# Two-block transformer kernel: the first input projection on the input without the tokens' factors, with softplus moved to GpSimd

## The chip, the core and the metric

The kernel is one program on one core of a Trainium2 chip. The metric is device time in microseconds of one execution. Engines: PE (TensorE, matrix products), DVE (VectorE), ACT (ScalarE), POOL (GpSimd), SP (SyncE, which here only issues DMAs). Each engine works through its own instructions in order; semaphores join them.

## The reference, cut to what matters

Two blocks run on 256 tokens of width 1024, all in fp32. The part that is touched is the first block up to its output projection:

```python
def rms_norm(x, w):
    xf = x.astype(jnp.float32)
    y = xf * lax.rsqrt(jnp.mean(xf * xf, axis=-1, keepdims=True) + EPS)
    return (y * w.astype(jnp.float32)).astype(x.dtype)

xn = rms_norm(h, mix_norm_w[l])
proj = jnp.einsum('bsd,de->bse', xn, w_in[l])
q, f_logit, i_v, g, lru_x, lru_gate = jnp.split(proj, ...)
# hgrn2_mix
qf = silu(q);  f = lb + (1 - lb) * sigmoid(f_logit);  log_f = log(f);  k = 1 - f
# per chunk of 32 tokens, b = cumsum(log_f):
#   q*exp(b), k*exp(-b), k*exp(b_last - b), scores, state;  then a group norm, times silu(g)
# rglru_mix
r, ig = sigmoid(block products of conv(lru_x));  log_a = -LRU_C * r * softplus(-a_param)
a = exp(log_a);  h = scan(a, sqrt(1 - a*a) * ig * xc);  y = h * gelu(lru_gate)
h = h + einsum('bse,ed->bsd', concat(o_hg, o_lru), w_out)
```

Behind it come a gated feed-forward network, a second block with two kinds of attention, and a mixture of 16384 single-neuron experts, for which each token's chosen rows are gathered from memory. The factor rsqrt(mean(x*x)) of a token multiplies all of that token's products, so it may be applied before a projection or behind it.

## The kernel before

**Layout.** Activations lie with features on the 128 partitions and 256 tokens along the free dimension. `hT` is the input, eight tiles of 128x256. A projection is one product per weight unit: a unit is 128x1024 fp32 (512 KB), eight blocks for the eight input tiles, and gives 128 output features. For precision every fp32 operand is split in two fp32r parts. ACT writes the high part of a unit to `whi` (L1004, `split` in `act`), DVE writes what remains to `ring_lo` (L1484, `split` in `dve`). Tiles are split in the same manner into `xhi` and `xlo`. A unit costs 24 products: eight of high by high (L437), eight of high by the input's rest (L440), eight of the weight's rest by high (L465, L466, or L454 in the first product of a stage).

**What sets the order.** Everything is written out by hand; each engine's program is in `act`, `dve`, `pe`, `pool` and `sync`. Weight units are split ahead by `Lookahead`: `whi` holds six units, so the first six (names `U_f` and the first two of `U_qq`) are split by `fill(1)` to `fill(3)`, and each later pair when `take` is called for a pair that TensorE is through with. A `take(U)` therefore splits the pair that stands three pairs further on: `take(U_f[2:4])` splits `U_qq[2:4]`, `take(U_qq[0:2])` splits `U_lx[0:2]`, and so on. `take` stands in ACT's program and in DVE's, at places of their own, and neither engine goes on before its two splits are issued.

**The stages of the touched part.** (1) ACT squares `hT`, DVE adds six of the squares, TensorE sums over the features (`sums`), ACT makes the token factors `rstd` (L1018, L1023), DVE scales the input to `xn` (L1511), and then both split it (L1029, L1504). TensorE issues filler products (`keep_clock`, L431) before and behind. (2) TensorE runs six gemms of two units each: f 0 and 1 (the forget logits), qq 0 and 1 (queries), lx 0 and 1 (the recurrent branch's input). ACT reads f and qq from PSUM with a sigmoid (L1083, L1087) and lx with a copy (L1105). DVE makes `ff` (L1577), 23 small steps of the softplus of `lru_a` (L1587 to L1598), `kk` (L1600), two memsets for the scan's chunk limits (L1602, L1604), the scan over the logarithm of f (L1610) and the decayed queries and keys, the last of which is `ks` (L1622). (3) TensorE waits for `ks`, transposes it (L554), makes the scores (L562), the token-major product v (L482 to L484), the gates (L594), and then lg 0, lg 1, g 0 and g 1 with the recurrence of the states between them. (4) The recurrent branch ends with `y` (L1693); its four tiles are split into `ahi` (L1150) and `alo` (L1699), with which the output projection begins (`residual`, `first(0)`). Between its first and second pair stands `hg_norm`: two sums (L624) over `sq`, the squares of the other branch's output (L1158).

**SyncE** issues the loads: four pieces of `hT`, constants, the vectors `vv` with all norm weights, then units in the order of use, each when its ring slot is free.

## Time and profile before

| what | value |
|---|---|
| median of 3 runs | 1137.63 us (1137.52 to 1138.79) |
| the profiled execution | 1137.43 us |
| its span (first to last instruction) | 1135.5 us |
| outside the span | 1.9 us |
| granted TensorE clock, mean | 0.978 |
| PE busy | 1018.7 us, 90% |
| DVE busy | 850.7 us, 75% |
| ACT busy | 419.9 us, 37% |
| POOL busy | 289.9 us, 26% |

The span falls in two parts. Up to about 490 us the two blocks are computed, with TensorE busy nearly throughout. Behind that the experts' rows are gathered, and DMA carries 420 GB/s to the end. The touched part is the first 139 us: the first product of the feed-forward network stands at 139.2 us. Shares of busy time say little about it; what counts is when TensorE has nothing to do and whom it waits for.

### The profile page before, as it was taken

How to read it: one execution, taken by the hardware profiler on the slowest of the kernel's cores; microseconds unless marked ns; L12 is line 12 of the kernel's file. 1: busy time of each engine (PE TensorE's matmuls, PEld its weight loads, DVE VectorE, ACT ScalarE, POOL GpSimd, SP SyncE). 2: the span in 40 equal slices, each digit the busy share in tenths (PEclk: the TensorE clock that was granted, in tenths of full speed). 3: DMA queues.
4: the chain of work that ended last, by engine and by line, in shares of the span. 5: the costliest groups of instructions: out<-in, count | busy, mean ns of one | idle time of the engine just before them, and what ended most of it. 6: DMA issues, size and time to landing. Idle time of an engine off the chain costs nothing.

```text
span 1135.5 us, 14403 instructions
## 1 busy us (share of the span) xinstructions
PE 1018.7 (90%) x5146; PEld 711.0 (63%) x5146; DVE 850.7 (75%) x1789; ACT 419.9 (37%) x839; POOL 289.9 (26%) x262
## 2 busy tenths in 40 slices
PE   7999999999999999999999998787867887767896
PEld 7999999999998877966655554233323333223342
DVE  6988699999867984686797776776776677677555
ACT  5646544445356654352322231221221122122121
POOL 0000000000000000144555544444444444445440
PEclk9999999999999999999999999989999999998999
DMA  9633479889828334599999999999999999999995
GB/s 358 223 136 106 149 256 360 329 302 334 308 77 326 138 112 154 224 381 421 422 420 420 422 420 421 422 421 421 421 422 422 421 422 421 422 421 422 420 422 215
DMA packets 68183, 378.61 MB, mean 333 GB/s; under 512 B 7568, under 2 KB 7952, under 8 KB 35600
## 3 DMA queue, kind: packets, MB, share of 16 engines
q0 software_dynamic: 37152, 268.45, 57.0%
q1 hardware_dynamic: 29808, 106.09, 25.4%
q10 hardware_dynamic: 1152, 3.15, 0.8%
q8 instruction: 42, 0.69, 0.3%
q14 instruction: 29, 0.24, 0.1%
HBM read 376.61 MB, written 1.05 MB: 333 GB/s over the span
## 4 chain that ended last, share of the span: by engine, by line
PE 51%; DMA 32%; DVE 11%; ACT 3%; issue 2%; SPq 0%; POOL 0%; DVEq 0%; ACTq 0%; POOLq 0%
DMA ring_sb<-in_peer,idsb 32%; PE pb L437 8%; PE pb L440 8%; PE pb L940 7%; PE pb L943 7%; PE pb L465 5%; DVE ring_lo L1484 2%; PE pb L894 2%; DVE ring_sb L2179 2%; PE pb L655 2%; PE pb L880 2%; PE pb L819 1%; PE pb L466 1%; PE pb L484 1%; PE pb L482 1%
## 5 line engine op out<-in xcount | busy, mean ns | idle before, releaser
L2179 DVE CUSTOM_DVE_ANT_0 ring_sb<-ring_sb,arena 128x1024 f32<-128x1024 f32 x138 | 168.8, 1224 | 73.5 <-DMA ring_sb<-in_peer,idsb 72.2
L940 PE MATMUL pb<-ring_sb,arena 128*128 128x512 f32 x276 | 153.5, 639 | 74.0 <-ACT arena L1418 74.0
L2280 POOL DMA_INDIRECT ring_sb<-in_peer,idsb x136 | 155.8, 1146 | 213.0 <-PE pb L943 190.2
L437 PE MATMUL pb<-xhi,whi 128*128 128x256 f32 x704 | 178.8, 289 | 2.9 <-DVE arena L1913 2.0
L2280 POOL DMA_INDIRECT arena<-in_peer,idsb x38 | 41.6, 1094 | 539.6 <-DVE idsb L2070 475.0
L440 PE MATMUL pb<-xlo,whi 128*128 128x256 f32 x704 | 175.8, 285 | 0.2
L1413 ACT ACTIVATE arena<-arena 128x4 f32<-128x4 f32 (+2 forms) x77 | 15.7, 205 | 432.2 <-DVE arena L2179 432.1
L1484 DVE TENSOR_TENSOR ring_lo<-ring_sb,whi 128x1024 fp32r<-128x1024 f32 x126 | 147.5, 1217 | 11.2 <-ACT whi L1004 11.1
L943 PE MATMUL pb<-ring_sb,arena 128*128 128x512 f32 x276 | 148.8, 622 | 0.0
L940 PEld LDWEIGHTS pb<-ring_sb,arena 128*128 128x128 f32 x276 | 52.0, 200 | 146.6 <-issue 145.5
L437 PEld LDWEIGHTS pb<-xhi,whi 128*128 128x128 f32 x704 | 134.7, 191 | 6.9 <-issue 3.2
L440 PEld LDWEIGHTS pb<-xlo,whi 128*128 128x128 f32 x704 | 134.8, 191 | 2.6 <-issue 1.4
L1004 ACT ACTIVATE whi<-ring_sb 128x1024 fp32r<-128x1024 f32 x126 | 125.3, 1047 | 9.8 <-DMA ring_sb<-in_w_down 8.7
L943 PEld LDWEIGHTS pb<-ring_sb,arena 128*128 128x128 f32 x276 | 55.7, 202 | 72.0 <-issue 72.0
L1418 ACT ACTIVATE arena<-cs,arena 128x128 f32<-128x128 f32 x256 | 83.2, 391 | 19.4 <-DVE arena L2185 19.1
L2179 DVE CUSTOM_DVE_ANT_0 whi_rows<-whi_rows,arena 128x1024 f32<-128x1024 f32 x39 | 47.7, 1224 | 46.9 <-DMA whi_rows<-in_peer,idsb 46.9
L465 PE MATMUL pb<-xhi,ring_lo 128*128 128x256 f32 x546 | 78.3, 283 | 0.1
L465 PEld LDWEIGHTS pb<-xhi,ring_lo 128*128 128x128 f32 x546 | 71.1, 192 | 0.3 <-DVE ring_lo L1484 0.3
L2179 DVE CUSTOM_DVE_ANT_0 arena<-arena 128x1024 f32<-128x1024 f32 x38 | 46.5, 1223 | 23.9 <-DMA arena<-in_peer,idsb 23.5
L940 PE MATMUL pb<-arena 128*128 128x512 f32 x76 | 41.5, 629 | 22.1 <-ACT arena L1418 22.1
L440 PE MATMUL pb<-alo,whi 128*128 128x256 f32 x208 | 58.2, 285 | 0.8 <-DVE alo L1699 0.8
L437 PE MATMUL pb<-ahi,whi 128*128 128x256 f32 x208 | 58.5, 286 | 0.0
(393 smaller groups left out, 1781.8 us busy)
## 6 DMA issues: line engine op xcount, KB each, us to landing
ring_sb<-in_ada SPq DMA_DIRECT2D x48, 512.0 KB, 5.5
ring_sb<-in_w_gu SPq DMA_DIRECT2D x44, 512.0 KB, 6.8
ring_sb<-in_w_in SPq DMA_DIRECT2D x38, 512.0 KB, 7.7
ring_sb<-in_w_down SPq DMA_DIRECT2D x22, 512.0 KB, 5.9
ring_sb<-in_w_out SPq DMA_DIRECT2D x16, 512.0 KB, 3.5
ring_sb<-in_w_q SPq DMA_DIRECT2D x8, 512.0 KB, 4.0
whi_rows<-in_w_q SPq DMA_DIRECT2D x6, 512.0 KB, 9.3
ring_sb<-in_peer,idsb POOLq DMA_INDIRECT x136, 27.2
```

The costliest lines, as they stand in the source:

```text
L437: e.matmul(o, hi_w(u)[:, c], xh(k), start=start, stop=False, skip_group_check=skip)
L440: e.matmul(o, hi_w(u)[:, c], xl(k), start=False, stop=False, skip_group_check=skip)
L465: e.matmul(o, lo_w(u)[:, kc(k)], hi_of(k), start=False, stop=False)
L655: mm = e.matmul(o, lo_w(u)[:, kc(n)], ah_of(k), start=False, stop=False, skip_group_check=True)
L880: mm = e.matmul(pb[b][:, j * 128:(j + 1) * 128], slot(u)[:, kc(k)], xk(k)[:, tile * 128:(tile + 1) * 128], start=k == 0 and j == 0, stop=k ...
L940: mm = e.matmul(pb[4 + 2 * tile][:, :], dgr[col % 8], o[:, 1024:1536], start=begin, stop=end)
L943: e.matmul(pb[5 + 2 * tile][:, :], dgr[col % 8], o[:, 1536:2048], start=begin, stop=end).then_inc(*PU.up(("row", col)))
L1004: e.activation(hi_w(u), slot(u), ACT.Copy).then_inc(*HI.up(u))
L1418: e.activation(dgr[col % 8], c_("ident"), ACT.Copy, scale=ae[:, col:col + 1]).then_inc(*AD.up(("dg", col)))
L1484: e.tensor_tensor(lo_w(u), slot(u), hi_w(u).bitcast(F32), SUB).then_inc(*LOV.up(u))
L2179: e.tensor_tensor_reduce(o, o, h2t[tile], 1.0, 0.0, MUL, ADD, aa[:, col:col + 1]).then_inc(*VD.up(("dot", col)))
L2280: e.indirect_dma_start(rows_at[s], None, peer, bass.IndirectOffsetOnAxis(ap=idsb[:, col:col + 1], axis=0)).then_inc(s_row[s], 16)
```

## The change

- The first six gemms, and v, lg and g, multiply `hT` times the norm weight, without the token factors. Where such a product leaves PSUM, it is multiplied by the token factor: `scaled` on DVE for f, qq, lx, lg and g (one instruction of 128x512 each), and a per-partition scale in ACT's copy for v, for which TensorE turns the factors into token-major form (`rtok0`). ACT's sigmoids for f, qq and g read the scaled copy in SBUF and no longer PSUM; ACT's copies of lx and lg are gone.
- The norm weight `mix` comes in front of the input, in the same load, as `hx`. ACT makes `xhi` by a copy with that scale, DVE makes `xlo` in one instruction. The sums over the squares move into the middle of gemm f 1, and take five products in place of three (DVE adds four squares, not six). The eight filler products behind them are gone; the ten in front stay.
- ACT computes `ff` (before: DVE), and the logarithm ahead of the queries' sigmoids, which now wait for a third table load.
- The softplus steps run on GpSimd, but for one reciprocal on DVE, and so do the memset of `scT` and the two memsets for the scan. DVE's scan waits for the last of these.
- The factor 0.5 of the GELU is folded into the product that gives `y`. The split of `y` stands ahead of both halves of g on ACT and DVE.
- SyncE issues the second part of the constants and the positions four units later.

```diff
-                e.dma_start(half(hT, i), half(xT, i)).then_inc(s_x[i], 16)
+                cols = slice(KD + 512 * i if i else 0, KD + 512 * (i + 1))
+                e.dma_start(hx[:, cols], xT[:, cols]).then_inc(s_x[i], 16)
...
+                        product(o, u, kc(k), k, hi_of, lo_of, k == 0, False, (paced, k) if paced and i == 0 else False)
...
-            sums("n0", (0, 8), (AN, ("n0", "ln")))
+            def first_sums():
+                e.wait_ge(s_cst, 16)
+                sums("n0", (0, 0), (AN, ("n0", "ln")))
+
+            gemm(U_f[0:2], ("f", 0), (VH, ("fx", 0)), paced="n0")
+            gemm(U_f[2:4], ("f", 1), (VH, ("fx", 1)), mid=first_sums)
+            gemm(U_qq[0:2], ("qq", 0), (VH, ("qx", 0)))
+            gemm(U_qq[2:4], ("qq", 1), (VH, ("qx", 1)))
...
-            gemm(U_f[0:2], ("f", 0), (AH, ("sf", 0)), fresh="n0")
-            gemm(U_f[2:4], ("f", 1), (AH, ("sf", 1)))
...
+            b = where["rtok0"] = bank((AN, "rtok0"))
+            e.wait_ge(*AN.at(("n0", "rstd")))
+            for tile in range(2):
+                mm = e.matmul(pb[b][:, tile:tile + 1], rstd[:, tile * 128:tile * 128 + 128], c_("ident")[:, 0:1], start=True, stop=True)
+            mm.then_inc(*PN.up("rtok0"))
...
+            first = la.fill(1)
...
+                e.activation(hi_of(k), hk(k), ACT.Copy, scale=mix[:, k:k + 1]).then_inc(*XHI.up(("n0", k)))
+                if k == 1:
+                    split(first[0:1])
+            split(first[1:2])
+            for k in range(KD):
                 square("n0", k)
+            split(la.fill(2))
+            split(la.fill(3))
...
-            x_hi("n0")
...
             for i in range(2):
+                e.wait_ge(*VH.at(("fx", i)))
+                e.activation(half(sf, i), half(sf, i), ACT.Sigmoid).then_inc(*AH.up(("sf", i)))
+                if i == 0:
+                    e.wait_ge(*VH.at("oml"))
+                e.wait_ge(*AH.at(("sf", i)))
+                for h in (2 * i, 2 * i + 1):
+                    e.activation(one_(ff, h), one_(sf, h), ACT.Identity, scale=oml[:, h:h + 1], bias=lbd[:, h:h + 1]).then_inc(*AH.up(("ff", h)))
                 take(U_f[2 * i:2 * i + 2])
...
-                e.activation(half(sf, i), pb[where["f", i]][:, :], ACT.Sigmoid).then_inc(*AH.up(("sf", i)))
...
             e.activation(lf, ff, ACT.Ln).then_inc(*AH.up("lf"))
+            take(U_qq[0:2])
...
+            e.preload_act_table_set(SIGM)
+            for i in range(2):
+                e.wait_ge(*VH.at(("qx", i)))
+                e.activation(half(qs, i), half(qdec, i), ACT.Sigmoid).then_inc(*AH.up(("qs", i)))
+            take(U_qq[2:4])
...
-                e.activation(half(vtok, tile), pb[where["v"][tile]][:, :], ACT.Copy).then_inc(*AH.up(("v", tile)))
...
+                e.activation(half(vtok, tile), pb[where["v"][tile]][:, :], ACT.Copy, scale=rtok0[:, tile:tile + 1]).then_inc(*AH.up(("v", tile)))
...
+            take(U_g[0:2])
+            e.wait_ge(*VL.at("y"))
...
+                    take(U_g[2:4])
+                e.wait_ge(*VH.at(("gx", i)))
+                e.activation(half(gs, i), half(lg, i), ACT.Sigmoid).then_inc(*AH.up(("gs", i)))
...
+            def scaled(dst, bank_, st_, name):
+
+                rs = one_(rstd, 0).unsqueeze(1).broadcast_to([128, 2, T])
+                e.tensor_tensor(v3(dst, T), v3(pb[bank_][:, :], T), rs, MUL).then_inc(*st_.up(name))
...
+                e.scalar_tensor_tensor(out=lo_of(k), in0=hk(k), scalar=mix[:, k:k + 1], in1=hi_of(k).bitcast(F32), op0=MUL,
+                                       op1=SUB).then_inc(*XLO.up(("n0", k)))
+                if k == 1:
+                    split(first[0:1])
+            split(first[1:2])
...
-            e.memset(scT, 0.0).then_inc(*VH.up("sc0"))
...
+            split(la.fill(3))
+            e.wait_ge(*AN.at(("n0", "rstd")))
+            e.wait_ge(*USED.at(U_f[1]))
+            scaled(half(sf, 0), where["f", 0], VH, ("fx", 0))
+            e.wait_ge(*GL.at("two more"))
+            e.reciprocal(sp_acc, sp_acc).then_inc(*VH.up("softr"))
...
+            e.wait_ge(*USED.at(U_f[3]))
+            scaled(half(sf, 1), where["f", 1], VH, ("fx", 1))
...
-            e.wait_ge(*PN.at("n0"))
-            e.memset(sq[:, 0:1024], 1.0).then_inc(*VH.up("m1"))
-            e.wait_ge(*VH.at("m1"))
-            e.memset(sq[:, 0:1024:CH], 0.0).then_inc(*VH.up("m0"))
...
+            e.wait_ge(*AH.at("lf"))
+            e.wait_ge(*GL.at("m0"))
+            e.tensor_tensor_scan(bb, sq[:, 0:1024], lf, 0.0, MUL, ADD).then_inc(*VH.up("bb"))
+            take(U_f[2:4])
...
+            e.wait_ge(*USED.at(U_qq[1]))
+            scaled(half(qdec, 0), where["qq", 0], VH, ("qx", 0))
+            take(U_qq[0:2])
...
+            e.wait_ge(*USED.at(U_qq[3]))
+            scaled(half(qdec, 1), where["qq", 1], VH, ("qx", 1))
+            take(U_qq[2:4])
+            for i in range(2):
+                e.wait_ge(*AH.at(("qs", i)))
+                e.tensor_tensor(half(qs, i), half(qdec, i), half(qs, i), MUL).then_inc(*VH.up(("qs", i)))
...
+                e.wait_ge(*USED.at(U_lg[2 * i + 1]))
+                scaled(x_, where["lg", i], VL, ("lg", i))
...
-            e.tensor_tensor(th_, th_, gx, MUL).then_inc(*VL.up("y"))
+            e.scalar_tensor_tensor(out=th_, in0=gx, scalar=0.5, in1=th_, op0=MUL, op1=MUL).then_inc(*VL.up("y"))
+            take(U_g[0:2])
...
+                e.wait_ge(*USED.at(U_g[2 * i + 1]))
+                scaled(half(lg, i), where["g", i], VH, ("gx", i))
+                if i == 0:
+                    take(U_g[2:4])
                 e.wait_ge(*AH.at(("gs", i)))
-                e.tensor_tensor(half(gs, i), pb[where["g", i]][:, :], half(gs, i), MUL).then_inc(*VH.up(("gs", i)))
...
+            e.memset(scT, 0.0).then_inc(*GL.up("sc0"))
+            e.wait_ge(*AH.at("su"))
+
+            def soft(ins, name):
+                ins.then_inc(*GL.up(name))
+                e.wait_ge(*GL.at(name))
+
+            soft(e.tensor_scalar(sp_acc, su, 2.0, None, ADD), "two more")
+            e.wait_ge(*VH.at("softr"))
+            soft(e.tensor_tensor(su, su, sp_acc, MUL), "ratio")
...
+            for d in (13, 11, 9, 7, 5, 3, 1):
+                soft(e.tensor_tensor(sp_acc, sp_acc, w2_, MUL), ("times", d))
+                soft(e.tensor_scalar(sp_acc, sp_acc, 1.0 / d, None, ADD), ("term", d))
...
+            soft(e.tensor_scalar(nsp, sp, -LRU_C, None, MUL), "nsp")
+            e.wait_ge(*PN.at("n0"))
+            soft(e.memset(sq[:, 0:1024], 1.0), "m1")
+            soft(e.memset(sq[:, 0:1024:CH], 0.0), "m0")
```

The first place is on DVE, between the first half of `ff` and the transposes' operand `ks`. `arena` holds nearly all tiles of this stage, `sq` the scan's chunk limits; two 128x1024 rows at `ring_lo` are the rests of one pair of units. In the kernel before, at the first half of `ff`:

```order
L1577 TENSOR_SCALAR arena<-arena,small 128x256 [waits s_dve_hgrn,s_act_hgrn]
L1577 TENSOR_SCALAR arena<-arena,small 128x256
L1484 TENSOR_TENSOR ring_lo<-ring_sb,whi 128x1024 [waits s_hi_split] x2
L1577 TENSOR_SCALAR arena<-arena,small 128x256 [waits s_act_hgrn]
L1577 TENSOR_SCALAR arena<-arena,small 128x256
L1587 TENSOR_SCALAR small<-small 128x4 [waits s_act_hgrn]
```

The pair at L1484 is that of qq 1; it stands ahead of the second half of `ff` and of all softplus steps, of which L1587 is the first. Behind the softplus DVE goes on:

```order
L1604 MEMSET sq 128x32 [waits s_dve_hgrn]
L1484 TENSOR_TENSOR ring_lo<-ring_sb,whi 128x1024 [waits s_hi_split,s_dve_hgrn]
L1484 TENSOR_TENSOR ring_lo<-ring_sb,whi 128x1024 [waits s_hi_split]
L1615 TENSOR_TENSOR arena<-pb,arena 128x512 [waits s_act_hgrn]
L1618 TENSOR_TENSOR small<-small,vv 128x8 [waits s_act_hgrn]
L1484 TENSOR_TENSOR ring_lo<-ring_sb,whi 128x1024 [waits s_hi_split] x2
L1610 SCALAR_TENSOR_TENSOR arena<-sq,arena 128x1024 [waits s_act_hgrn]
L1613 TENSOR_TENSOR arena<-arena 128x1024 [waits s_dve_hgrn]
L1615 TENSOR_TENSOR arena<-pb,arena 128x512 [waits s_act_hgrn]
L1620 TENSOR_TENSOR arena<-arena 128x1024 [waits s_act_hgrn]
L1622 TENSOR_TENSOR arena<-arena 128x1024 [waits s_act_hgrn]
```

The pairs here are lx 0 and lx 1, both ahead of the scan (L1610); `ks` is L1622. The same stretch of DVE in the changed kernel:

```order
L1494 TENSOR_TENSOR ring_lo<-ring_sb,whi 128x1024 [waits s_hi_split] x2
L1552 TENSOR_TENSOR arena<-pb,rstd 128x512 [waits s_unit_used,s_act_norm]
L1594 RECIPROCAL small<-small 128x4 [waits s_pool_lru]
L1596 CAST cosT<-arena 128x256 [waits s_pos]
L1598 TENSOR_TENSOR small<-small,vv 128x8 [waits s_act_hgrn]
L1552 TENSOR_TENSOR arena<-pb,rstd 128x512 [waits s_unit_used]
L1603 TENSOR_SCALAR arena<-arena 128x1024 [waits s_act_hgrn]
L1606 SCALAR_TENSOR_TENSOR arena<-sq,arena 128x1024 [waits s_pool_lru,s_act_hgrn]
L1494 TENSOR_TENSOR ring_lo<-ring_sb,whi 128x1024 [waits s_hi_split] x2
L1610 TENSOR_TENSOR arena<-arena 128x1024 [waits s_dve_hgrn]
L1552 TENSOR_TENSOR arena<-pb,rstd 128x512 [waits s_unit_used]
L1494 TENSOR_TENSOR ring_lo<-ring_sb,whi 128x1024 [waits s_hi_split] x2
```

The pair ahead of L1552 is qq 0. That of qq 1 has moved behind the scan (L1606), which waits for GpSimd and for the logarithm, and that of lx 0 is the last row; `ff` is gone from DVE and the reads from PSUM (L1552) have come in.

The second place is on ACT, between the split of `y` (`ahi`) and the logarithm for the group norm's factors (`stdt`). Before:

```order
L1004 ACTIVATE whi<-ring_sb 128x1024 [waits s_slot11,s_unit_used]
L1004 ACTIVATE whi<-ring_sb 128x1024 [waits s_slot12,s_unit_used]
L1150 ACTIVATE ahi<-xn 128x256 [waits s_dve_lru]
L1150 ACTIVATE ahi<-xn 128x256 x3
L1154 ACTIVATE arena<-pb 128x512 [waits s_unit_used]
L1155 ACT_TABLE_LOAD
L1158 ACTIVATE sq<-pb 128x512 [waits s_pe_hgrn]
L1158 ACTIVATE sq<-pb 128x512
L1004 ACTIVATE whi<-ring_sb 128x1024 [waits s_slot13,s_unit_used]
L1004 ACTIVATE whi<-ring_sb 128x1024 [waits s_slot14,s_unit_used]
L1163 ACTIVATE stdt<-pb,cs 128x512 [waits s_pe_hgrn]
```

Both sigmoids of g (L1154) wait for their gemm, and the pair of splits that `take(U_g[2:4])` issues stands at the top. In the changed kernel:

```order
L1159 ACTIVATE ahi<-xn 128x256 [waits s_dve_lru]
L1159 ACTIVATE ahi<-xn 128x256 x3
L1164 ACTIVATE arena<-arena 128x512 [waits s_dve_hgrn]
L1013 ACTIVATE whi<-ring_sb 128x1024 [waits s_slot11,s_unit_used]
L1013 ACTIVATE whi<-ring_sb 128x1024 [waits s_slot12,s_unit_used]
L1164 ACTIVATE arena<-arena 128x512 [waits s_dve_hgrn]
L1165 ACT_TABLE_LOAD
L1168 ACTIVATE sq<-pb 128x512 [waits s_pe_hgrn]
L1168 ACTIVATE sq<-pb 128x512
L1013 ACTIVATE whi<-ring_sb 128x1024 [waits s_slot13,s_unit_used]
L1013 ACTIVATE whi<-ring_sb 128x1024 [waits s_slot14,s_unit_used]
L1173 ACTIVATE stdt<-pb,cs 128x512 [waits s_pe_hgrn]
```

Each sigmoid (L1164) now waits for a DVE instruction, and that pair stands between the two. The third place is the same stretch on DVE. Before:

```order
L1693 TENSOR_TENSOR xn<-xn,sq 128x1024 [waits s_dve_lru]
L1484 TENSOR_TENSOR ring_lo<-ring_sb,whi 128x1024 [waits s_hi_split] x2
L1701 TENSOR_TENSOR arena<-pb,arena 128x512 [waits s_act_hgrn]
L1484 TENSOR_TENSOR ring_lo<-ring_sb,whi 128x1024 [waits s_hi_split] x2
L1699 TENSOR_TENSOR alo<-xn,ahi 128x256 [waits s_x_hi] x4
L1701 TENSOR_TENSOR arena<-pb,arena 128x512 [waits s_act_hgrn]
L1484 TENSOR_TENSOR ring_lo<-ring_sb,whi 128x1024 [waits s_hi_split] x2
L1706 SCALAR_TENSOR_TENSOR arena<-pb,vv,rstd 128x512 [waits s_act_hgrn]
```

The four `alo` rows, for which the output projection waits, stand behind two pairs and one half of g. In the changed kernel:

```order
L1698 SCALAR_TENSOR_TENSOR xn<-sq,xn 128x1024 [waits s_dve_lru]
L1494 TENSOR_TENSOR ring_lo<-ring_sb,whi 128x1024 [waits s_hi_split] x2
L1702 TENSOR_TENSOR alo<-xn,ahi 128x256 [waits s_x_hi] x4
L1552 TENSOR_TENSOR arena<-pb,rstd 128x512 [waits s_unit_used]
L1494 TENSOR_TENSOR ring_lo<-ring_sb,whi 128x1024 [waits s_hi_split] x2
L1709 TENSOR_TENSOR arena<-arena 128x512 [waits s_act_hgrn]
L1552 TENSOR_TENSOR arena<-pb,rstd 128x512 [waits s_unit_used]
L1709 TENSOR_TENSOR arena<-arena 128x512 [waits s_act_hgrn]
L1494 TENSOR_TENSOR ring_lo<-ring_sb,whi 128x1024 [waits s_hi_split] x2
L1714 SCALAR_TENSOR_TENSOR arena<-pb,vv,rstd 128x512 [waits s_act_hgrn]
```

They moved up past one pair and that half; both halves of g now stand behind them, each as a read from PSUM (L1552) and a product with the sigmoid (L1709), with ACT's sigmoid between the two.

## Rows read from the trace of the kernel before

**Rows 1.** The page: PE's busy tenths, the chain's shares, one group of part 5.

```profile
PE   7999999999999999999999998787867887767896
...
PE 51%; DMA 32%; DVE 11%; ACT 3%; issue 2%; SPq 0%; POOL 0%; DVEq 0%; ACTq 0%; POOLq 0%
...
L2280 POOL DMA_INDIRECT ring_sb<-in_peer,idsb x136 | 155.8, 1146 | 213.0 <-PE pb L943 190.2
```

**Rows 2.** Windows: from:to, its length, busy us (count) by engine, PEclk, DMA, GB/s.

```profile
20.70:49.50 28.80, 28.68 (x240) 28.48 (x238) 26.75 (x60) 17.38 (x23) 0.00 (x0) 1.00 0.80 305
...
104.00:109.00 5.00, 4.18 (x35) 3.98 (x34) 5.00 (x8) 2.61 (x5) 0.00 (x0) 1.00 0.53 154
...
139.00:330.00 191.00, 190.92 (x1594) 190.41 (x1592) 169.42 (x214) 89.19 (x127) 0.00 (x0) 1.00 0.80 292
```

**Rows 3.** Timeline of PE, first 15 us: start, length, line, out<-in, count, [idle before].

```profile
5.38 4.64 PE L431 MATMUL pb<-hT 128*128 128x128 f32 x20 [5.38 <-DMA hT<-in_xT]
...
11.18 1.19 PE L496 MATMUL pb<-sq,cs 128*128 128x256 f32 x4
...
14.50 0.36 PE L437 MATMUL pb<-xhi,whi 128*128 128x256 f32 x1 [0.35 <-ACT xhi L1029]
```

**Rows 4.** Timeline of ACT, first 30 us.

```profile
12.40 0.47 ACT L1018 ACTIVATE stdt<-pb,cs 128x256 f32<-128x256 f32 x1 [0.44 <-PE pb L496]
...
19.23 3.89 ACT L1004 ACTIVATE whi<-ring_sb 128x1024 fp32r<-128x1024 f32 x4
...
26.48 1.28 ACT L1079 ACT_TABLE_LOAD   x1
27.78 0.60 ACT L1083 ACTIVATE arena<-pb 128x512 f32<-128x512 f32 x1
```

**Rows 5.** Timeline of DVE, 33 to 46 us.

```profile
33.69 0.16 DVE L1593 TENSOR_TENSOR small<-small 128x4 f32<-128x4 f32 x1
33.89 0.17 DVE L1594 TENSOR_SCALAR small<-small 128x4 f32<-128x4 f32 x1
...
36.90 0.70 DVE L1600 TENSOR_SCALAR arena<-arena 128x1024 f32<-128x1024 f32 x1
37.75 0.91 DVE L1602 MEMSET sq<- 128x1024 f32 x1 [0.16 <-issue]
...
41.16 0.68 DVE L1615 TENSOR_TENSOR arena<-pb,arena 128x512 f32<-128x512 f32 x1
...
44.10 2.28 DVE L1610 TENSOR_TENSOR_SCAN arena<-sq,arena 128x1024 f32<-128x1024 f32 x1
```

**Rows 6.** Timeline of POOL, first microsecond: its only instructions before the gathers.

```profile
0.27 0.10 POOL L2367 MEMSET const-float32-1.0<- 128x1 f32 x1
```

**Rows 7.** Timeline of PE, at the waits for `ks`, for `alo`, and at the group norm's sums.

```profile
50.57 1.09 PE L554 MATMUL pb<-cs,arena 128*128 128x128 f32 x8 [0.55 <-DVE arena L1622]
...
108.70 0.39 PE L440 MATMUL pb<-alo,whi 128*128 128x256 f32 x1 [0.82 <-DVE alo L1699]
...
111.84 1.88 PE L624 MATMUL pb<-sq,cs 128*128 128x512 f32 x4
```

**Rows 8.** Timeline of DVE, 101 to 110 us.

```profile
101.96 1.22 DVE L1693 TENSOR_TENSOR xn<-xn,sq 128x1024 f32<-128x1024 f32 x1
103.09 2.35 DVE L1484 TENSOR_TENSOR ring_lo<-ring_sb,whi 128x1024 fp32r<-128x1024 f32 x2
...
108.23 1.42 DVE L1699 TENSOR_TENSOR alo<-xn,ahi 128x256 fp32r<-128x256 f32 x4
```

**Rows 9.** Timeline of ACT, 103 to 110 us.

```profile
108.81 1.09 ACT L1158 ACTIVATE sq<-pb 128x512 f32<-128x512 f32 x2
```

**Rows 10.** Timeline of PE, two gaps in the gather part.

```profile
736.12 1.10 PE L940 MATMUL pb<-arena 128*128 128x512 f32 x2 [2.63 <-ACT arena L1418]
...
746.05 2.05 PE L940 MATMUL pb<-ring_sb,arena 128*128 128x512 f32 x2 [2.83 <-ACT arena L1418]
```

**Rows 11.** Window behind the second of those gaps.

```profile
745.30:748.70 3.40, 2.65 (x3) 1.18 (x4) 2.50 (x9) 1.28 (x4) 0.54 (x1) 0.51 1.01 422
```

160 lines of the change are left out of this document (56 added, 104 removed).

## The prediction, made before the changed kernel was run

> **What bounds the kernel now.** I read the page first. Its busy tenths of PE and its chain [rows 1] show TensorE full in the first half of the span and the gathers' DMA in the second, so I looked at where the touched part, the first 139 us, leaves TensorE without work. The windows answer it: from 20.7 to 49.5 us it is busy for 28.68 of 28.8 us, at 104 to 109 us it lacks 0.8 us, and from 139 to 330 us it is busy for 190.92 of 191 [rows 2]. The timeline names the gaps: nothing useful before the first weight product at 14.50 us [rows 3], 0.55 us before the transposes at 50.57 us, 0.82 us before the first product with `alo` at 108.70 us [rows 7]. So the stretch behind 14.5 us is bound by TensorE's own work, with ACT and DVE close behind. Since the feed-forward network goes on without a gap and the gathers wait for its results, I carry a shift at 139 us to the end one to one. The profiled execution took 1137.43 us, its span and 1.9 us around it; the median is 0.2 us longer. A measurement of this kernel can tell about 0.2% (2.3 us) from no change.
>
> **The gain at the start.** The ten filler products stay, and end at 10.0 us (5.38 + 4.64) [rows 3]. `xhi`, `xlo` and the first split unit need only the input's first pieces and are there by then, so weight products start at 10.0 instead of 14.5 us: 4.5 us gained. Given back: until about 11.2 us TensorE runs at half speed (there four records of 256 columns begin to take 1.0 us [rows 3], half of what they took before), 0.6 us; and five fp32 sums of 256 columns now stand inside gemm f 1. A 512-column sum takes 0.88 us here (1.88 for two with the tail) [rows 7], so five of half the size take 2.15 us. If nothing waited, the transposes would start near 10.0 + 0.6 + 6 x 5.76 + 2.15 + 0.1 = 47.4 us, 3.2 us earlier than now. (A gemm is 48 products; 240 fill 28.8 us [rows 2], 0.12 us each.)
>
> **The first wait that takes its place.** The rests of qq 1 now stand behind DVE's scan, so I follow the chain to the scan.
> - TensorE: f 0 ends at 16.4, f 1's first unit at 19.2, the sums at 21.5 us with their tail.
> - ACT: logarithm and exponential of the factors 0.47 and 0.45 [rows 4], three exponentials of four columns, by my estimate from DVE's 0.16 us for such a tile [rows 5] 0.35 together: 22.8 us.
> - DVE: four small dependent steps at 0.20 (33.69 to 33.89) [rows 5], 23.5; the pair of qq 0, 2.27 (two of 2.35 with one tail [rows 8]), 25.8; the scaled read from PSUM, 0.68 [rows 5]: 26.5 us.
> - ACT: the sigmoid, 0.60 [rows 4], 27.1; two tiles of `ff`, each priced like the factors' logarithm of the same size, 0.47 less a tail of 0.1, the second sigmoid and two more tiles: 29.2; the high parts of qq 1, 3.89/4 = 0.97 each [rows 4], 31.15; the table load, 1.28 [rows 4], 32.4; the logarithm of 1024 columns, priced like a split unit, 1.05: 33.5 us.
> - DVE: the scan, 2.21 of issue (2.28 with its tail) [rows 5], then qq 1's first rest, 1.22: 37.0 us.
>
> TensorE gets to qq 1 at 30.3 us and has used its high part at 32.2 us. It then stands until 37.0 us: 4.8 us. The 32 products left (3.84) and both lx gemms (11.52) give 52.4 us; with `rtok0` the transposes start at 52.5 us, 1.9 us later than now. `ks` is ready before that (about 44.3 us), so today's 0.55 us wait is gone and hides nothing any more. The high part of lx 1 comes at 46.6 us, just when it is wanted. **Term: +1.9 us.**
>
> **Softplus on GpSimd.** It starts behind DVE's reciprocal at 26.6 us, makes 22 dependent steps and the memsets, and must be through by 33.5 us, or the scan waits, with qq 1's rests queued behind it and TensorE waiting for those. With 1.1 us for the memsets (0.91 on DVE [rows 5]) the limit is (33.5 - 26.6 - 1.1)/22 = 0.26 us a step. No row shows GpSimd arithmetic. Bounds: a one-column memset's 0.10 us [rows 6] from below, which costs nothing; an indirect DMA's 1.15 us [rows 1] from above, 22 x 0.89 = +19.5 us. The nearest row in kind is DVE's 0.20 us [rows 5]; I take half more, 0.30 us, as each step also passes a semaphore. **Term: +0.8 us**, and 2.2 us for each further 0.1 us. What DVE is freed of (23 x 0.2 = 4.6 us, one memset of 0.91 us twice) gains nothing, because DVE then waits for the logarithm.
>
> [...]
>
> **TensorE's clock.** Behind a gap of 2.83 us at 746 us the granted clock is 0.51 in the first window [rows 11], the 1.2 GHz level, and a pair of products takes 2.05 us instead of 1.10; behind a gap of 2.63 us at 736 us it does not fall [rows 10]. A gap of 4.8 us is longer than both. A stretch of 3.4 us at the lower level, as in that window, loses 1.7 us of work; the bounds are 0 and twice that. I take the middle, since TensorE is then dense up to the transposes. **Term: +1.7 us.** The Trainium skill, "TensorE: Matmul & The Clock Gate", part 1, says the throttled state is the default and only activity lifts it; by that rule the fall is certain, by the rows likely, and the sum differs by this term.
>
> **The end of the recurrent branch.** From lg on TensorE is dense again; DVE reads lg with a scale (0.68 us) where ACT copied it (0.60), so `y` keeps its distance. From the start of `y` the sums of the group norm now start 9.9 us later (101.96 to 111.84) [rows 7, 8]: they wait for `alo`, 0.82 us, and the rest of TensorE's work. After the change `alo` comes 2.9 us sooner, and TensorE is through with the first pair about 1 us sooner. But `sq` comes later. From the start of `y`: 1.14, one pair 2.27, four `alo` 1.34, the scaled g 0 0.68 (5.5 in all with the issue overlaps), ACT's sigmoid and the first of two high parts to 7.1, DVE's pair 2.27, the product with the sigmoid 0.60 and the scaled g 1 0.69 to 10.65, sigmoid 0.5, table 1.28 [rows 4] and the square 0.6 [rows 9]: 13.0 us. **Term: +3.1 us**, and a gap of about 4.6 us on TensorE. Behind it ACT has a pair of high parts (1.9 us) queued ahead of the group norm's logarithm; before, that pair was done while ACT waited. The second half of `xlo` then comes 9.7 us behind the sums instead of 8.3. **Term: +1.4 us.** A fallen clock in that gap costs little, as TensorE has slack there: **+0.3 us.**
>
> **Sum:** 1137.43 + 1.9 + 0.8 + 1.7 + 3.1 + 1.4 + 0.3 = 1146.6 us, against the median 1146.8 us.
>
> **The rivals.**
> - The softplus decides (0.15): steps of 0.5 us or more. At 0.6 us the scan waits 7.5 us instead of 0.8: 1153.5 us. For it: 23 instructions with a semaphore each on an engine whose indirect DMAs take 1.15 us. Against: the memsets of 0.10 us.
> - Mild (0.17): a softplus in time and no fallen clock: 1137.6 + 1.9 + 3.1 + 1.4 = 1144.0 us.
> - Faster (0.04): the rests of qq 1 are there when TensorE asks, and `sq` when the first pair is done. Then only 3.2 us at the start and 0.8 us at `alo` count: 1133.6 us. It needs a scan that starts by 32.2 - 1.2 - 2.2 = 28.8 us, before `ff` is whole by my count. For it speaks only that a wait in a hand-written order is easily misplaced by me.
> - No change (0.03): the first wait alone is absent: -3.2 + 3.1 + 1.4 gives 1138.9 us.
>
> **How the numbers follow.** The forecast has 0.61. The range goes from 1142 us, a little under the mild case, to 1154 us, which takes in steps of 0.6 us; about 0.1 is left above and 0.07 below. Faster 0.04, within 0.2% 0.03, slower 0.93.
>
> **What would show it.** Right: weight products from 10 us; a gap of 4 to 7 us on PE inside qq 1, released by DVE's `ring_lo`; scan at 33 to 36 us; transposes near 55 us; a gap of 4 to 5 us before the group norm's sums, released by ACT; the feed-forward network's first product near 148 us. Wrong: scan before 30 us, GpSimd's `m0` far from 34 us, or a shift at 139 us that shrinks in the gather part.

## The result, and the profile after

| | before | after |
|---|---|---|
| median of 6 runs each | 1137.91 us (1137.52 to 1138.79) | 1147.65 us (1146.42 to 1149.13) |
| profiled execution | 1137.43 us | 1147.03 us |
| its span | 1135.5 us | 1145.1 us |
| its mean granted clock | 0.978 | 0.973 |

The change costs 0.84% (ratio 1.0084, 95% interval 1.0074 to 1.0095). The forecast was 1146.8 us in a range of 1142 to 1154, so 0.85 us separate it from the median. The profiled executions lie 9.60 us apart. Both add about 1.9 us to their spans, so the rows can be compared directly.

The page of the kernel after: its part 1, the busy tenths of PE and the chain.

```profile
PE 1023.8 (89%) x5138; PEld 713.1 (62%) x5138; DVE 845.5 (74%) x1758; ACT 420.4 (37%) x840; POOL 298.5 (26%) x288
...
PE   7799899999999999999999998777877877787797
...
PE 43%; DMA 32%; DVE 17%; ACT 4%; issue 3%; POOL 1%; POOLq 0%; DVEq 0%; SPq 0%; ACTq 0%
```

PE's tenths are nearly as full as before [rows 1]; PE's share of the chain fell from 51% to 43%, DVE's rose from 11% to 17%. PE is busy 5 us longer (1023.8 against 1018.7) with no more products (5138 against 5146), which points to the clock. The place of the loss is in PE's timeline (start, length, line, operation, count, idle before it and what ended it):

```profile
5.88 4.63 PE L435 MATMUL pb<-hx 128*128 128x128 f32 x20 [5.88 <-DMA hx<-in_xT]
10.17 0.56 PE L441 MATMUL pb<-xhi,whi 128*128 128x256 f32 x1
...
30.97 0.35 PE L441 MATMUL pb<-xhi,whi 128*128 128x256 f32 x1 [0.86 <-ACT whi L1013]
...
38.15 1.86 PE L469 MATMUL pb<-xhi,ring_lo 128*128 128x256 f32 x7 [5.05 <-DVE ring_lo L1494]
...
55.44 1.07 PE L563 MATMUL pb<-cs,arena 128*128 128x128 f32 x8
...
119.88 3.63 PE L633 MATMUL pb<-sq,cs 128*128 128x512 f32 x4 [4.79 <-ACT sq L1168]
```

Against [rows 3, 7]: the weight products start at 10.17 instead of 14.50 us. Then TensorE waits 0.86 us for the high part of qq 1, stands 5.05 us in the middle of qq 1's first unit for `ring_lo` from DVE, and starts the transposes at 55.44 us, 4.87 us later than before. It stands again, for 4.79 us, before the group norm's sums (L633), for ACT's squares. The windows (from:to, length, busy us and count by engine, PEclk, DMA, GB/s) show what follows each gap:

```profile
38.10:41.50 3.40, 3.35 (x15) 3.35 (x16) 3.40 (x4) 1.10 (x2) 0.00 (x0) 0.50 0.10 17
...
120.00:123.40 3.40, 3.40 (x5) 1.32 (x6) 2.21 (x2) 3.31 (x5) 0.00 (x0) 0.50 0.00 0
148.00:330.00 182.00, 181.61 (x1508) 181.02 (x1507) 162.86 (x197) 83.02 (x117) 0.00 (x0) 1.00 0.84 307
```

In 38.1 to 41.5 us TensorE is busy for 3.35 us and does 15 products; the clock is at 0.50, its 1.2 GHz level. The same in 120.0 to 123.4 us. From 148 us on it is dense, as before [rows 2]. DVE, ACT and GpSimd around the first gap:

```profile
29.91 0.69 DVE L1603 TENSOR_SCALAR arena<-arena 128x1024 f32<-128x1024 f32 x1 [2.60 <-ACT arena L1101]
34.69 2.29 DVE L1606 TENSOR_TENSOR_SCAN arena<-sq,arena 128x1024 f32<-128x1024 f32 x1 [4.09 <-POOL sq L2290]
36.90 2.33 DVE L1494 TENSOR_TENSOR ring_lo<-ring_sb,whi 128x1024 fp32r<-128x1024 f32 x2
```

```profile
29.78 1.99 ACT L1013 ACTIVATE whi<-ring_sb 128x1024 fp32r<-128x1024 f32 x2
...
33.08 1.06 ACT L1105 ACTIVATE arena<-arena 128x1024 f32<-128x1024 f32 x1
```

```profile
26.61 0.20 POOL L2277 TENSOR_TENSOR small<-small 128x4 f32<-128x4 f32 x1 [3.49 <-DVE small L1594]
...
30.11 0.57 POOL L2282 TENSOR_SCALAR small<-small 128x4 f32<-128x4 f32 x1
...
33.43 0.95 POOL L2289 MEMSET sq<- 128x1024 f32 x1
```

DVE makes `kk` at 29.91 us, then waits 4.09 us for GpSimd's mask, scans at 34.69 us, and only then makes the rests of qq 1 (L1494, x2). At the end of the branch ACT and DVE read so:

```profile
112.52 2.00 ACT L1013 ACTIVATE whi<-ring_sb 128x1024 fp32r<-128x1024 f32 x2
...
117.84 1.28 ACT L1165 ACT_TABLE_LOAD   x1
119.13 1.08 ACT L1168 ACTIVATE sq<-pb 128x512 f32<-128x512 f32 x2
120.10 2.00 ACT L1013 ACTIVATE whi<-ring_sb 128x1024 fp32r<-128x1024 f32 x2
122.00 0.69 ACT L1173 ACTIVATE stdt<-pb,cs 128x512 f32<-128x512 f32 x1
```

```profile
106.51 1.22 DVE L1698 SCALAR_TENSOR_TENSOR xn<-sq,xn 128x1024 f32<-128x1024 f32 x1
...
116.47 0.68 DVE L1552 TENSOR_TENSOR arena<-pb,rstd 128x512 f32<-128x512 f32 x1
...
129.00 0.76 DVE L1720 TENSOR_TENSOR xlo<-arena,xhi 128x256 fp32r<-128x256 f32 x2 [0.48 <-ACT xhi L1180]
```

All the profiled executions side by side. "qq 1" is the start of its first product, "distance" from there to the transposes, `y`, "sums" and `xlo` the starts of DVE's `y`, of the group norm's sums and of the second half of `xlo`, "FFN" the first product of the feed-forward network; all in us of the span. The last column is the median of the timed runs.

| kernel | qq 1 | transposes | distance | `y` | sums | `xlo` | FFN | median |
|---|---|---|---|---|---|---|---|---|
| before | 32.20 | 50.57 | 18.37 | 101.96 | 111.84 | 119.82 | 139.23 | 1137.9 to 1138.3 |
| after | 30.97 | 55.44 | 24.47 | 106.51 | 119.88 | 129.00 | 148.45 | 1147.65 |
| e12_fill_gap | 30.06 | 53.16 | 23.10 | 104.22 | 117.59 | 126.71 | 146.46 | 1145.22 |
| e2_limits_first | 31.09 | 55.48 | 24.39 | 106.53 | 119.90 | 129.02 | 148.79 | 1145.34 |
| e13_ten_steps | 30.39 | 57.83 | 27.44 | 108.91 | 122.27 | 131.40 | 150.84 | 1149.33 |
| e1_rests_early | 30.18 | 52.86 | 22.68 | 103.92 | 117.29 | 126.41 | 146.37 | 1145.61 |
| e3_early_limits | 31.36 | 51.80 | 20.44 | 102.85 | 116.22 | 125.33 | 145.46 | 1143.59 |
| e7_start | 31.25 | 49.10 | 17.85 | 100.18 | 113.54 | 122.66 | 142.07 | 1140.59 |
| e5_squares_first | 31.25 | 55.98 | 24.73 | 107.04 | 115.66 | 128.55 | 150.28 | 1148.46 |
| e10_end2 | 30.16 | 55.61 | 25.45 | 106.68 | 115.30 | 125.06 | 145.11 | 1143.64 |
| e11_both2 | 30.07 | 47.91 | 17.84 | 98.98 | 107.61 | 117.35 | 137.39 | 1137.53 |
| e14_early_clock | 30.21 | 48.06 | 17.85 | 99.11 | 107.73 | 117.48 | 138.54 | 1136.47 |
| e15_both3 | 30.04 | 47.88 | 17.84 | 98.95 | 107.57 | 117.22 | 136.61 | 1135.76 |
| e16_before_gpsimd | 32.14 | 49.42 | 17.28 | 100.34 | 110.22 | 118.19 | 137.61 | 1136.39 |

Two remarks for reading it. From the same code TensorE reaches qq 1 at 30.04 to 30.39 us in some executions and at 30.97 to 31.36 us in others, so differences of a step are taken from the distances and not from single clock times. And the median of five runs is only good to about 1 us for these kernels, whose runs lie 1.6 to 3.6 us apart and were not timed side by side with the kernel after; where a few tenths are at stake, the rows decide.

### The profile page after: what moved, and what is told of

It reads as the page before. It is cut to its first block, busy times and chain, and to the rows that moved or that the text cites. A ratio compares the mean times of both kernels' runs of the same rounds, so it can differ in the third digit from the quotient of the medians.

```text
span 1145.1 us, 14390 instructions
## 1 busy us (share of the span) xinstructions
PE 1023.8 (89%) x5138; PEld 713.1 (62%) x5138; DVE 845.5 (74%) x1758; ACT 420.4 (37%) x840; POOL 298.5 (26%) x288
## 4 chain that ended last, share of the span: by engine, by line
PE 43%; DMA 32%; DVE 17%; ACT 4%; issue 3%; POOL 1%; POOLq 0%; DVEq 0%; SPq 0%; ACTq 0%
DMA ring_sb<-in_peer,idsb 21%; PE pb L949 8%; DMA xn<-in_peer,idsb 7%; PE pb L952 7%; PE pb L441 5%; PE pb L444 5%; DVE ring_lo L1494 5%; PE pb L469 3%; DMA ring_sb<-in_peer,halves 2%; PE pb L903 2%; DVE arena L1756 2%; DVE ring_sb L2188 1%; PE pb L889 1%; PE pb L828 1%; PE pb L664 1%
## 5 line engine op out<-in xcount | busy, mean ns | idle before, releaser
L949 PE MATMUL pb<-ring_sb,arena 128*128 128x512 f32 x276 | 150.4, 627 | 71.2 <-ACT arena L1428 71.1
L2312 POOL DMA_INDIRECT ring_sb<-in_peer,idsb x136 | 151.9, 1117 | 205.2 <-PE pb L952 183.5
L1494 DVE TENSOR_TENSOR ring_lo<-ring_sb,whi 128x1024 fp32r<-128x1024 f32 x126 | 147.9, 1219 | 16.8 <-ACT whi L1013 16.6
L952 PE MATMUL pb<-ring_sb,arena 128*128 128x512 f32 x276 | 148.4, 621 | 0.0
L1013 ACT ACTIVATE whi<-ring_sb 128x1024 fp32r<-128x1024 f32 x126 | 125.2, 1046 | 12.9 <-DMA ring_sb<-in_w_down 9.2
L469 PE MATMUL pb<-xhi,ring_lo 128*128 128x256 f32 x560 | 81.4, 285 | 5.4 <-DVE ring_lo L1494 5.4
L469 PEld LDWEIGHTS pb<-xhi,ring_lo 128*128 128x128 f32 x560 | 73.5, 193 | 5.8 <-DVE ring_lo L1494 5.8
L2188 DVE CUSTOM_DVE_ANT_0 arena<-arena 128x1024 f32<-128x1024 f32 x38 | 46.5, 1224 | 23.8 <-DMA arena<-in_peer,idsb 23.3
```

Source lines behind the costliest of these rows:

```text
L469: e.matmul(o, lo_w(u)[:, kc(k)], hi_of(k), start=False, stop=False)
L949: mm = e.matmul(pb[4 + 2 * tile][:, :], dgr[col % 8], o[:, 1024:1536], start=begin, stop=end)
L952: e.matmul(pb[5 + 2 * tile][:, :], dgr[col % 8], o[:, 1536:2048], start=begin, stop=end).then_inc(*PU.up(("row", col)))
L1013: e.activation(hi_w(u), slot(u), ACT.Copy).then_inc(*HI.up(u))
L1494: e.tensor_tensor(lo_w(u), slot(u), hi_w(u).bitcast(F32), SUB).then_inc(*LOV.up(u))
L2188: e.tensor_tensor_reduce(o, o, h2t[tile], 1.0, 0.0, MUL, ADD, aa[:, col:col + 1]).then_inc(*VD.up(("dot", col)))
```

## The experiments

The theory is that of the prediction: the changed kernel waits at two places because of the order in which DVE, ACT and GpSimd work their queues off, and the clock falls behind both waits. The rivals: the gain at the start is not there in the first place (input later, half speed, sums inside f 1); GpSimd decides; or what is won at one place is lost before the feed-forward network.

### The clock in the first gap

```diff
                         product(o, u, kc(k), k, hi_of, lo_of, ...)
+                    for _ in range(18 if u == U_qq[2] else 0):
+                        e.matmul(pb[7][:, 0:128], c_("ones"), c_("ones"), start=True, stop=True, skip_group_check=True)
                     e.wait_ge(*rest_of(u))
```

> The changed kernel with 18 filler products of 128 columns (0.24 us each, 4.3 us together, on constants into an unused bank; their result is not used) put where TensorE waits for the rests of qq 1, between 32.9 and about 37.3 us. Nothing else moves: the rests still come at 38.15 us. Theory A (the granted clock falls because TensorE stands, and this costs by itself): at full speed up to 41.5 us TensorE does in those 3.41 us twice the work; 1.7 us are won, the transposes start at 53.7 us, the time is 1145.9 us. Theory B (the clock's fall costs nothing since the lx gemms wait for their high parts anyway): within 0.5 us of the changed kernel, 1147.2 us or more.

Measured: 1145.22 us (1144.53 to 1148.04), ratio 1.0069 (1.0055 to 1.0083). PE's timeline in and behind the gap:

```profile
32.04 4.18 PE L468 MATMUL pb<-cs 128*128 128x128 f32 x36
37.25 1.10 PE L471 MATMUL pb<-xhi,ring_lo 128*128 128x256 f32 x7 [1.03 <-DVE ring_lo L1496]
```

The fillers stand in the gap, the rests come 7.19 us behind qq 1's first product as they did without fillers (7.18 us), the next seven products take 1.10 us instead of 1.86, and the distance falls from 24.47 to 23.10 us. So the fallen clock cost 1.37 us by itself, and theory B falls. The scatter of the times is as large as that, so the time alone would not have shown it.

### How GpSimd weighs on the scan

```diff
             e.memset(scT, 0.0).then_inc(*GL.up("sc0"))
+            e.wait_ge(*PN.at("n0"))
+            soft(e.memset(sq[:, 0:1024], 1.0), "m1")
+            soft(e.memset(sq[:, 0:1024:CH], 0.0), "m0")
             e.wait_ge(*AH.at("su"))
...
             soft(e.tensor_scalar(nsp, sp, -LRU_C, None, MUL), "nsp")
-            e.wait_ge(*PN.at("n0"))
-            soft(e.memset(sq[:, 0:1024], 1.0), "m1")
-            soft(e.memset(sq[:, 0:1024:CH], 0.0), "m0")
```

> The changed kernel, with GpSimd's two memsets of the scan's mask put ahead of the softplus, so that the scan waits for no softplus. Theory A (GpSimd finished 0.5 us behind ACT's logarithm: scan at 34.69 us, logarithm done at 34.14 us): the scan starts at 34.2 us, 0.5 us earlier, the gap in qq 1 becomes 0.5 us shorter, the time 1147.1 us, within what can be told. Theory B (GpSimd's share is larger: its work beside DVE slows DVE and delays the logarithm's inputs too): the scan before 33.5 us, the time under 1146 us.

Measured: 1145.34 us (1144.77 to 1146.97), ratio 1.0063 (1.0049 to 1.0077). The rows agree with theory A: the scan starts 3.21 us behind qq 1's first product instead of 3.72, now released by the logarithm, and the gap is 4.52 us instead of 5.05.

```profile
34.30 2.29 DVE L1606 TENSOR_TENSOR_SCAN arena<-sq,arena 128x1024 f32<-128x1024 f32 x1 [3.57 <-ACT arena L1105]
...
37.76 1.86 PE L469 MATMUL pb<-xhi,ring_lo 128*128 128x256 f32 x7 [4.52 <-DVE ring_lo L1494]
```

The distance still falls by 0.08 us only, because in this execution the clock stayed at 0.50 from about 35.3 to 42 us and took 1.8 us. The median is 2.3 us lower than that of the kernel after and would be theory B's, but its sign, a scan before 33.5 us, is not there. The rows explain 0.5 us, and the profiled execution is the slowest of its five; what the rest is, is not shown.

Ten more steps of the kind of the softplus between it and the mask:

```diff
+            for i in range(10):
+                soft(e.tensor_scalar(w2_, w2_, 1.0, None, MUL), ("more", i))
             e.wait_ge(*PN.at("n0"))
             soft(e.memset(sq[:, 0:1024], 1.0), "m1")
```

> The changed kernel with ten more small dependent steps on GpSimd between the softplus and the scan's mask. Theory A (GpSimd decides the scan's start, each step costs 0.31 us, and everything behind the scan follows one to one): the scan at 34.69 + 3.1 = 37.8 us, the gap in qq 1 about 8.1 us, the time 1147.6 + 3.1 = 1150.7 us. Theory B (there is slack behind the scan's start, or the steps are shorter without their semaphores than the records suggest): less than 2 us.

Measured: 1149.33 us (1148.46 to 1150.67), ratio 1.0098 (1.0083 to 1.0114).

```profile
32.87 2.96 POOL L2289 TENSOR_SCALAR small<-small 128x4 f32<-128x4 f32 x10
...
40.62 1.65 PE L469 MATMUL pb<-xhi,ring_lo 128*128 128x256 f32 x6 [8.09 <-DVE ring_lo L1494]
```

Ten steps last 3.02 us, the gap grows by 3.04 us and the distance by 2.97. Theory A holds in the rows: GpSimd was on the path, one to one. The time shows less: the median is 1.7 us above that of the kernel after, which by itself would be theory B's, and those two medians are good to about 1 us.

### The rests ahead of the scan

```diff
             e.tensor_scalar(kk, ff, -1.0, 1.0, MUL, ADD).then_inc(*VH.up("kk"))
+            take(U_f[2:4])
             e.wait_ge(*AH.at("lf"))
             e.wait_ge(*GL.at("m0"))
             e.tensor_tensor_scan(bb, sq[:, 0:1024], lf, 0.0, MUL, ADD).then_inc(*VH.up("bb"))
-            take(U_f[2:4])
```

> The changed kernel, with DVE's two rests of the second query pair (qq 1) taken ahead of the scan instead of behind it. Theory A (the price of the first gap is the queue order on DVE, and the fallen clock follows from the gap): DVE is idle from 30.6 to 34.7 us in the changed kernel, so the rests come at about 31 to 33.5 us and the 5.05 us gap at 38.15 us disappears. In its place TensorE waits about 2.7 us for the rests of lx 0 (behind scan and `d`) and about 1.7 us for the high part of lx 1, by walking the queues with the durations of the rows. The transposes then start 2.2 us earlier than the changed kernel's 55.44 us from the queues alone, and 1.7 us more if the granted clock stays at full speed behind these shorter gaps: 51.5 us, and the time about 1143.7 us (1147.6 - 3.9). Theory B (DVE's order is not what holds it; the gap is bound by the logarithm and softplus, and any order of DVE's work shows the same loss): within 0.5 us of the changed kernel. Theory C (the clock falls anyway behind gaps of 2.7 and 1.7 us): 1145.4 us.

Measured: 1145.61 us (1143.66 to 1146.77), ratio 1.0066 (1.0052 to 1.008): half of what theory A gave. The gap in qq 1 is gone and the clock stays up, but the distance fell by 1.8 us, not 3.9. PE's and GpSimd's timelines:

```profile
40.97 1.10 PE L469 MATMUL pb<-xhi,ring_lo 128*128 128x256 f32 x7 [2.88 <-DVE ring_lo L1494]
...
46.67 0.36 PE L441 MATMUL pb<-xhi,whi 128*128 128x256 f32 x1 [1.62 <-ACT whi L1013]
```

```profile
29.33 0.57 POOL L2282 TENSOR_SCALAR small<-small 128x4 f32<-128x4 f32 x1
...
30.27 1.11 POOL L2282 TENSOR_SCALAR small<-small 128x4 f32<-128x4 f32 x1
31.46 1.03 POOL L2281 TENSOR_TENSOR small<-small 128x4 f32<-128x4 f32 x1
```

The two waits of 2.88 and 1.62 us come almost as large as expected, and behind the first the seven products take 1.10 us, full speed. So the time is that of theory C, but not for its reason, since the clock stayed up. The 2.2 us of theory A were a slip of size: by its own waits (5.05 less 2.7 less 1.7) the queues had only 0.65 us to give. A wait of 5.05 us became two of 4.50 us together, half a microsecond, and the clock gave the rest. But the scan starts 5.45 us behind qq 1's first product, later than before the move (3.72): two of GpSimd's steps last 1.11 and 1.03 us instead of 0.22 and 0.20, and they are the two that lie beside DVE's rests, which start at 30.07 us:

```profile
30.07 2.37 DVE L1494 TENSOR_TENSOR ring_lo<-ring_sb,whi 128x1024 fp32r<-128x1024 f32 x2 [0.25 <-ACT whi L1013]
35.63 2.29 DVE L1607 TENSOR_TENSOR_SCAN arena<-sq,arena 128x1024 f32<-128x1024 f32 x1 [3.19 <-POOL sq L2290]
```

That gives a new theory: the rests, taken ahead, slow down the softplus, on which the scan waits.

> The changed kernel with the rests of qq 1 ahead of the scan and the scan's mask ahead of the softplus, but the lx pairs left where they are. Taken ahead alone, the rests won 1.8 us of the distance from qq 1's first product to the transposes (24.47 to 22.68 us), and the mask ahead alone 0.1 us (24.39). Theory A (GpSimd's steps stand still beside DVE's rests, 1.11 and 1.03 us instead of 0.20 for the two beside the pair, so that the scan went from 34.69 - 30.97 = 3.7 to 35.63 - 30.18 = 5.5 us behind qq 1's first product and took back what the rests had won): with the mask out of the softplus's queue the scan starts at once behind the logarithm, 3.2 us behind qq 1's first product; the waits at lx 0 and lx 1 shrink from 2.88 and 1.62 us to about 0.8 and 1.6 us, the distance to 20.5 us, the time to 1147.6 - 4 = 1143.6 us, more than the two moves give apart. Theory B (the two moves add, 1.9 us in all, and the rest of the 6.6 us comes from the lx pairs alone): the distance 22.6 us, the time 1145.5 us.

Its edit is the two above together. Measured: 1143.59 us (1141.15 to 1144.7), ratio 1.0041 (1.0027 to 1.0055), the distance 20.44 us against 20.5 expected. The scan now waits for the logarithm and for nothing else:

```profile
34.57 2.29 DVE L1607 TENSOR_TENSOR_SCAN arena<-sq,arena 128x1024 f32<-128x1024 f32 x1 [0.96 <-ACT arena L1105]
...
39.91 1.10 PE L469 MATMUL pb<-xhi,ring_lo 128*128 128x256 f32 x7 [0.64 <-DVE ring_lo L1494]
```

Apart, the moves were worth 1.79 and 0.08 us; together 4.03. The 0.08 us hold a clock that cost 0.4 us more in e2's execution; by the gaps alone the moves were worth 0.55 and 0.53 us apart, and 2.80 together (5.05 less 0.64 less a wait of 1.61 at lx 1). Either way they do not add, and theory B falls.

### The whole first part

To those two moves this adds the lx pairs (ACT's part, then DVE's):

```diff
             take(U_qq[0:2])
+            take(U_qq[2:4])
             e.wait_ge(*VH.at("bb"))
             e.activation(kdec, bb, ACT.Exp, scale=-1.0).then_inc(*AH.up("enb"))
...
-            take(U_qq[2:4])
...
+            take(U_qq[0:2])
             e.wait_ge(*VH.at("bb"))
             bl = v3(bb, CH)[:, :, CH - 1:CH].broadcast_to([128, 32, CH])
...
             scaled(half(qdec, 0), where["qq", 0], VH, ("qx", 0))
-            take(U_qq[0:2])
```

> The changed kernel with three moves in its first part: the rests of qq 1 ahead of the scan on DVE, the scan's mask ahead of the softplus on GpSimd, and the lx pairs ahead of the steps that use the scan (ACT's high parts of lx 1 ahead of the three exponentials, DVE's rests of lx 0 ahead of `d`). Theory A (all that the changed kernel loses up to the transposes is queue order and the clock that falls in the gap): TensorE then stands nowhere between 10.5 us and the transposes, these start at about 48.3 to 49 us (55.44 - 6.5 - 0.5 at most from the queues, less what the clock gives back) instead of 55.44 and 50.57 in the kernel before; the time is 1147.6 - 6.6 to 8.3 = 1139.3 to 1141 us, with the 4.8 us gap at the group norm's sums unchanged. Theory B (the missing gain lies in the start itself: input 0.5 us later, half speed until 11.2 us, five sums inside f 1): the transposes stay behind 51 us and the time above 1143 us.

Measured: 1140.59 us (1139.42 to 1142.15, 11 runs), ratio 1.0019 (1.001 to 1.0028). The transposes start at 49.10 us, 6.34 us earlier than after and 1.47 us earlier than before, with no gap named from qq 1's first product at 31.25 us up to them:

```profile
49.10 1.07 PE L563 MATMUL pb<-cs,arena 128*128 128x128 f32 x8
```

All of it is still there at the feed-forward network (142.07 against 148.45 us). So there is a gain at the start, and theory B falls. It is 1.47 us here and 2.66 us in e11_both2 below, whose execution reached qq 1 1.2 us earlier; the sum had 3.2 us.

### The end of the recurrent branch

ACT's squares ahead of the second sigmoid:

```diff
-            for i in range(2):
-                if i:
-                    take(U_g[2:4])
-                e.wait_ge(*VH.at(("gx", i)))
-                e.activation(half(gs, i), half(lg, i), ACT.Sigmoid).then_inc(*AH.up(("gs", i)))
-            e.preload_act_table_set(LNEXP)
+            e.wait_ge(*VH.at(("gx", 0)))
+            e.activation(half(gs, 0), half(lg, 0), ACT.Sigmoid).then_inc(*AH.up(("gs", 0)))
+            take(U_g[2:4])
             e.wait_ge(*PH.at(("in", NCH - 1)))
             for hp in range(2):
                 e.activation(half(sq, hp), pb[6 + hp][:, :], ACT.Square).then_inc(*AH.up(("hsq", hp)))
+            e.wait_ge(*VH.at(("gx", 1)))
+            e.activation(half(gs, 1), half(lg, 1), ACT.Sigmoid).then_inc(*AH.up(("gs", 1)))
+            e.preload_act_table_set(LNEXP)
```

> The changed kernel, with ACT's squares for the group norm's sums put ahead of the second gate's sigmoid and ahead of the table load. TensorE's gap of 4.79 us before the sums then nearly goes: the sums start at about 115.9 us instead of 119.88. Theory A (what counts there is ACT's chain up to the logarithm of the sums, sigmoid, table and a pair of high parts, which is only put in another order; the gap before the sums is not itself the price): the logarithm starts at about 121 instead of 122.0 us, TensorE waits later instead, before the first product with `xhi`, about 2.5 us, and the time falls by 1 us, up to 2.7 us if the clock no longer falls: 1145 to 1146.6 us. Theory B (the gap before the sums is the price, as my sum had it): the time falls by 4 to 4.5 us, to about 1143.3 us.

Measured: 1148.46 us (1146.69 to 1149.16), ratio 1.0088 (1.0074 to 1.0102). The sums start 8.62 us behind `y` instead of 13.37, and nothing is won; the time is that of neither theory. ACT's and PE's timelines, and a window:

```profile
119.67 2.01 ACT L1013 ACTIVATE whi<-ring_sb 128x1024 fp32r<-128x1024 f32 x2
121.58 0.67 ACT L1173 ACTIVATE stdt<-pb,cs 128x512 f32<-128x512 f32 x1
```

```profile
128.57 0.58 PE L441 MATMUL pb<-xhi,whi 128*128 128x256 f32 x1 [2.38 <-ACT xhi L1180]
...
131.30:134.70 3.40, 3.40 (x19) 3.40 (x18) 0.76 (x2) 0.76 (x3) 0.00 (x0) 0.52 0.80 176
```

The table and the pair of high parts (L1013) now stand between the squares and the norm's logarithm at 121.58 us. From `y` to the second half of `xlo` it is 21.51 us instead of 22.49: the one microsecond of theory A. TensorE waits for `xhi` instead, 0.79 and then 2.38 us, and behind this the clock is at half, at 0.52 in 131.3 to 134.7 us. From `xlo` to the feed-forward network it is 21.73 us instead of 19.45, so the network comes 43.24 us behind `y`, where it was 41.94: the fallen clock took more than the order had won. So the gap before the sums was not itself the price, and theory B falls.

So the pair must get out of the logarithm's way. Besides this run's edit (squares, then the second sigmoid and the table):

```diff
                     e.activation(half(rstd, 0), half(stdt, 0), ACT.Exp, scale=-0.5).then_inc(*AH.up(("hr", hp)))
+                    split(new[hp:hp + 1])
                     e.wait_ge(*VH.at(("hg2", hp)))
...
+            split(pair[0:1])
+            e.wait_ge(*USED.at(U_g[3]))
+            scaled(half(lg, 1), where["g", 1], VH, ("gx", 1))
+            split(pair[1:2])
```

> The changed kernel, reordered at the end of the recurrent branch only. ACT: squares first, then the second sigmoid, table load, logarithm and exponential of the norm's first half, and only then the pair of high parts, one behind each exponential. DVE: the scaled read of g 1 between its two rests; the later pair's rests one behind each product with the gate. Theory A (the end costs 3.5 + 1.1 us and what the clock loses, all by queue order of ACT and DVE): the sums start at about 115.9 us, TensorE then waits 0.4, 1.3 and 0.7 us in short gaps, the feed-forward network starts 3.7 us earlier by the queues alone and 1.7 us more if the clock no longer falls: 1142.3 to 1144 us. Theory B (what is won there is given back before the feed-forward network, whose start the residual's chain sets): under 1.5 us.

Measured: 1143.64 us (1142.55 to 1144.14), ratio 1.0043 (1.0029 to 1.0057). The first `+` line stands in both ACT's and DVE's group norm. `y` to feed-forward network: 38.43 us, 3.51 less than after and 1.16 more than before (37.27). The three short gaps are 0.42, 1.13 and 0.49 us. Theory A holds, though the rows give the 3.5 us of the queues and no more for the clock; the shift reaches the end.

### Both, and what is left at the start

The edits of e7_start and e10_end2 together.

> Both reorderings together: the start's three moves (rests of qq 1 ahead of the scan, mask ahead of the softplus, lx pairs ahead of the exponentials and of `d`) and the end's (squares, sigmoid, table, logarithm, exponential, then high parts). Theory A (all of the change's loss is queue order and the clock behind the gaps): 1147.6 - 7.5 - 4.5 = 1135.6 us, 2.3 us under the kernel before, with the feed-forward network's first product at about 136.5 us. Theory B (the parts overlap: part of the start's gain is lost in a gap before the feed-forward network): 1138 us or more.

Measured: 1137.53 us (1135.93 to 1139.19, 11 runs), ratio 0.9993 (0.9984 to 1.0002): the whole loss of the change is gone, and with the change's computation as it is. The distance (17.84 us) and the stretch from `y` to the feed-forward network (38.41 us) are those of the two kernels apart (17.85 and 38.43 us), so nothing is lost between the parts. Of the forecast of 1135.6 us 1.9 are missing (the two kernels' medians, 7.1 and 4.0 us under that of the kernel after, add up to 1136.6); the feed-forward network starts at 137.39, not 136.5.

The next kernel takes the fillers from the input to GpSimd's zeros, from 1.7 us on:

```diff
-            e.wait_ge(s_x[0], 16)
-            keep_clock(10, hT[:, 0:128])
+            e.wait_ge(*GL.at("sc0"))
+            keep_clock(17, scT[:, 0:128])
```

> The kernel with both reorderings, and the ten filler products on the input's first tile replaced by 17 on the zeros that GpSimd writes at 0.7 to 1.7 us, so that TensorE works from about 2 us instead of from the input's landing at 5.8 us (the result of the fillers is not used in either). Theory A (the weight products' start is set by fillers at half speed, 0.46 us each, whose full speed comes at 9.4 us in some executions and at 10.6 to 11.5 us in others, as TensorE reached qq 1 at 30.1 us in five of the profiled executions and at 31.0 to 31.3 us in four; this is also why this kernel scatters over 3 us and the one before over 1.3): TensorE is at full speed when the input lands, the products start at 7.8 us, paced by ACT's high parts of the input (0.45 us each) until 11 us, TensorE reaches qq 1 at 29.8 us every time, the time is 1136.9 us (1137.5 - 0.6) and its runs lie within 1.5 us of one another. Theory B (the clock at the start is not what scatters): no change in either.

Measured: 1136.47 us (1135.22 to 1138.08, 11 runs), ratio 0.9982 (0.9973 to 0.9991). TensorE reaches qq 1 at 30.21 us, no sooner than in e11_both2 (30.07 us): the first products now wait for the input's parts, 0.46 us for `xlo` at 9.49 us. The runs still lie 2.9 us apart, not 1.5, so theory A is not borne out. In the slowest, which is the profiled one, the clock fell behind the gap of 1.12 us at 115.9 us (0.76 in 116 to 117 us, 0.50 in the next) and took about 1.0 us: `y` to feed-forward network is 39.43 us.

The last of this series adds another order inside the group norm (DVE shown; ACT in the same manner, `ln`, `exp`, `ln`, split, `exp`, split, then the high parts):

```diff
+                gain(0)
+                gated(0)
+                split(new[0:1])
+                gain(1)
+                gated(1)
+                split(new[1:2])
+                lo(0)
+                lo(1)
```

> As the run with the early fillers, and in the group norm ACT issues the second half's logarithm and exponential and both high parts ahead of the high parts of `eb`; DVE the second half's two products ahead of the rests of `eb`. Of the three short gaps (0.42, 1.12 and 0.49 us) one of about 1.1 us stays; by the queues 0.7 us are won: 1136.2 us, 0.17% under the kernel before. Against that: if the rest of the chain to the feed-forward network sets its start, nothing is won.

Measured: 1135.76 us (1135.04 to 1136.72, 11 runs), ratio 0.998 (0.9971 to 0.9989). This one is faster than both kernels, 0.2% under the kernel before, and its runs lie 1.7 us apart. `y` to feed-forward network is 37.66 us, 0.75 less than in e11_both2, as the queues had it.

PE's timeline, where the first weight product stands and at the two gaps that are left at the end:

```profile
7.67 0.39 PE L441 MATMUL pb<-xhi,whi 128*128 128x256 f32 x1 [0.21 <-ACT whi L1013]
...
112.99 0.36 PE L441 MATMUL pb<-ahi,whi 128*128 128x256 f32 x1 [0.60 <-ACT whi L1013]
...
116.68 0.74 PE L523 MATMUL pb<-ahi,ring_lo 128*128 128x256 f32 x4 [0.82 <-DVE ring_lo L1510]
```

### GpSimd's part alone, in the kernel before

> The kernel before, with only the GpSimd part of the change: softplus, the scan's mask and the clearing of `scT` on GpSimd (mask first, then softplus). DVE is freed of 4.6 + 1.8 us before its scan. Theory A (TensorE's own work bounds the kernel before; what DVE is freed of can only remove the 0.55 us wait for `ks`): the scan at about 41.5 instead of 44.1 us, the transposes at 50.0 us, the time 1137.4 us, a difference of 0.5 us which can't be told from none. Theory B (GpSimd's work beside DVE slows DVE, or the freed time reaches the end of the branch as well, where the first product with `alo` waits 0.82 us): 1136.5 us or less, or 1139 us or more.

Its edit, cut to DVE's side; the steps taken out stand in GpSimd's program as in the change, mask first:

```diff
-            e.memset(scT, 0.0).then_inc(*VH.up("sc0"))
...
-            soft(e.tensor_scalar(sp_acc, su, 2.0, None, ADD))
-            soft(e.reciprocal(sp_acc, sp_acc))
...
-            soft(e.tensor_scalar(nsp, sp, -LRU_C, None, MUL))
+            e.wait_ge(*GL.at("two more"))
+            e.reciprocal(sp_acc, sp_acc).then_inc(*VH.up("softr"))
...
-            e.memset(sq[:, 0:1024], 1.0).then_inc(*VH.up("m1"))
...
-            e.memset(sq[:, 0:1024:CH], 0.0).then_inc(*VH.up("m0"))
-            e.wait_ge(*VH.at("m0"))
+            e.wait_ge(*GL.at("m0"))
```

Measured: 1136.39 us (1135.19 to 1138.59, 11 runs), ratio 0.9985 (0.9976 to 0.9994). The time is theory B's, about 1.6 us instead of 0.5, by the median and by the feed-forward network's start. Its reasons are not borne out: the wait for `alo` is still 0.82 us, and DVE's scan takes 2.30 us beside GpSimd's steps, 2.28 before. What fell is theory A's limit, that only the 0.55 us could be won. DVE's scan and two of GpSimd's steps:

```profile
41.10 2.30 DVE L1588 TENSOR_TENSOR_SCAN arena<-sq,arena 128x1024 f32<-128x1024 f32 x1 [2.86 <-ACT arena L1094]
...
36.03 1.14 POOL L2255 TENSOR_TENSOR small<-small 128x4 f32<-128x4 f32 x1
...
41.37 2.02 POOL L2257 TENSOR_TENSOR small<-small 128x4 f32<-128x4 f32 x1
```

The scan comes at 41.10 instead of 44.10 us, the transposes at 49.42 instead of 50.57 us, and `y` 0.47 us closer behind them. Of the 1.15 us at the transposes, 0.55 is the wait for `ks` that I had named. Another 0.38 us is a wait too short for the timeline's bracket. Of the 0.47 us, 0.35 lies before the scores, which start 0.87 us behind the transposes instead of 1.22; in the kernel before, DVE's product for the queries (L1625, 50.43 us) ended just before them, at 51.65 us. About 0.3 us of the 1.62 has no row of its own. The last product of each of two units in the kernel before:

```profile
37.84 0.28 PE L466 MATMUL pb<-xhi,ring_lo 128*128 128x256 f32 x1
...
41.10 0.28 PE L466 MATMUL pb<-xhi,ring_lo 128*128 128x256 f32 x1
```

A unit takes 2.88 us, and in e16 these two products stand at 37.78 and 40.66 us; but in the kernel before lx 0's first unit took 3.26 us: its rests, from 38.88 us, lay behind softplus and mask on DVE. With DVE freed they were early, from 32.94 us. The softplus took long here, from 32.5 to 46.5 us: GpSimd's steps of 1.14 and 2.02 us lie beside DVE's rests and its scan. That cost nothing, because `nsp` isn't wanted before the gates.

This sets the whole change in its place. GpSimd's part alone took the kernel before to 0.9985 (0.9976 to 0.9994); all of the change with every reordering and the early fillers came to 0.998 (0.9971 to 0.9989). The intervals overlap, so it is not shown that the projection without the factors is worth anything on top of GpSimd's part; nor was the new order of the group norm tried in the kernel before.

## Why the prediction was right, step by step

**The gain at the start** came out, in part by luck: TensorE was ready for qq 1 at 30.11 us (30.97 less the wait of 0.86), against 30.3. The prediction's own terms give 30.03 (10.6 for the start, 17.28 for three gemms, 2.15 for the sums), so 30.3 is a small slip. Two more errors lie inside it and cancel: the input landed at 5.88 instead of 5.38 us, and full speed was back by about 10.7 us instead of 11.2. In the ten profiled executions in which the fillers wait for `hx` the input landed at 5.65 to 5.89 us, without `hx` at 5.32 and 5.38; that the norm weight in front of it is the cause lies near, but was not tried apart.

**A wait that I had not put in** is the 0.86 us for qq 1's high part. I had ACT through with `ff` at 29.2 us; it was at 29.8, mostly because a tile of `ff` was priced at 0.37 us and took 0.50 (the first two from 27.13 to 28.13 us). In the same stretch the two sigmoids took 0.72 and 0.65 us to the next start instead of 0.60.

**The first gap** was the step with the right mechanism and the right size: the rests stand behind the scan, and TensorE stood 5.26 us (7.18 less 1.92 for the 16 products), where stall and GpSimd term had given 5.6. The two terms were split wrongly by little: the logarithm was done at 34.14 us, not 33.5, so GpSimd's share was 0.5 us instead of 0.8. Its steps came 0.31 us apart, (33.43 - 26.61)/22, against 0.30 chosen. No row of before gave that 0.30; that it came so near is luck.

**The clock's term** of 1.7 us measured 1.37 in the profiled execution, and 1.3 to 2.3 us in four others with this gap (e2, e5, e10, e13), taken as the distance, less the 17.85 us that it takes without waits (e7), less the time stood. In every one of them the clock fell.

**Behind the transposes** `y` came 51.07 us later, 51.39 before: nearly the same distance, as said, and the 4.87 us became 4.55.

**The group norm's sums** came 13.37 us behind `y`, 3.49 more than before; the term was 3.1. Its steps are all there: g 1's scaled read is done 10.64 us behind `y`, as worked out (10.65); what is missing is the tails of the sigmoid and the square on ACT: 0.65 us to the table load instead of 0.5, and 0.75 us from the square's start to the sums' instead of 0.6.

**The pair ahead of the logarithm** cost 1.14 us (9.12 against 7.98 us from the sums to `xlo`) instead of 1.4; the prediction had 9.7 against 8.3, and its 8.3 is above the row. The term of 0.3 us for the fallen clock was hardly there: from `xlo` to the feed-forward network it is 19.45 us, 19.41 before. In the six other executions with the gap of 4.79 us it is 19.41 to 20.13.

Sum of the rows: 4.55 + 3.49 + 1.14 = 9.18 us at `xlo`, 9.22 at the feed-forward network, 9.60 at the end, against 9.2 in the sum. That it fits so closely is partly errors that cancel: up to `y` the sum had 4.4 us, behind it 4.8, and the rows have 4.55 and 4.67. The 0.4 us behind the feed-forward network lie within what the later part varies: from its first product to the end of the run it takes 998.2 to 1000.1 us in the profiled executions.

Where the sum misled was in what its terms would give back. I had priced each wait as if taking it away won its length. e1 and e5 show that it does not: behind the wait stood the next ones, 2.88 and 1.62 us in one case, 0.79 and 2.38 in the other. And "what DVE is freed of gains nothing" holds for the changed kernel only; in the kernel before it gained 1.6 us.

The Trainium skill, "TensorE: Matmul & The Clock Gate", part 1, has the throttled state as the default, released by activity, from which I had called the fall certain; it happened in both gaps of about 5 us. But behind 2.88 us (e1) it did not, and behind 2.38 us (e5) and once behind 1.12 us (e14) it did.

## What to carry to other kernels

When an engine that prepares operands for TensorE gets a new wait, look at what is queued behind it on that engine: here two rests whose high parts had been there for up to 6 us. Walk the queues again after each move and judge moves together, since two of them gave 1.9 us apart and 4.0 us together. Work given to GpSimd cost nothing where nobody waited for its end (e16), and its full length where the scan did (e13); beside DVE's large tiles that length grew. And try each part of a change by itself: here GpSimd's part was a gain that the rest of the change hid.

## What the hardware showed that I had not expected

**GpSimd stands still beside some DVE work.** A softplus step takes about 0.2 us alone and follows the one before by 0.28 to 0.31 us (DVE's own steps: 0.20 us). It takes 0.57 us beside `kk` (0.69 us, one operand in SBUF), 1.03 to 1.14 us beside the rests (two operands), 2.02 and 2.23 us beside the scan (e16, e7). Beside DVE's scaled read from PSUM at 26.63 us it stays at 0.20. DVE's instructions keep their length to 0.02 us (a pair of rests 2.37 instead of 2.35, the scan 2.30 instead of 2.28). The Trainium skill, "SBUF — State Buffer", section "SBUF: two separate sides", says that DVE and GpSimd share a pair of ports under an exclusive lock, which concerns a DVE instruction in a two-port mode or with two inputs in SBUF (the latter only against a GpSimd instruction that reads SBUF), and that the one that starts later blocks until the other is done. The rows agree: each long step started behind the DVE instruction beside it and ended within 0.1 us of its end.

**TensorE comes up to full speed at the start at different times.** The same 20 records of fillers on the input take 3.88 to 4.35 us in five executions and 4.63 or 4.64 in five others, and TensorE reaches qq 1 at 30.06 to 30.39 us and at 30.97 to 31.36 us. The speed is read from the records (0.23 us each here, 0.12 in e12's gap); PEclk reads 1.00 from the first microsecond on and does not show it. After the change this passes to the transposes. That it widens the scatter of the times is not shown: the 6 runs each lie 1.3 us apart before and 2.7 after, but 27 runs of the kernel before lie 2.9 us apart, and with early fillers it was 2.9 us (e14) and 1.7 (e15).

**The lower clock lasted 3.4 us in one execution and about 6.8 us in four others**, at the first gap (38.1 to 41.5 us after, above; about 35.3 to 42 us in e2_limits_first), so that nearly the same gap cost 1.4 us behind it in one case and 2.3 us in another (e10). A window of e2_limits_first:

```profile
36.00:42.00 6.00, 4.24 (x20) 4.24 (x21) 6.00 (x7) 3.20 (x4) 0.00 (x0) 0.50 0.24 62
```
